# Banded masks added by identity matmuls in a windowed-attention block, with three loads and steps moved

## The reference

```python
rel = kj - BLOCK - qi                                             # key pos - query pos
valid = (jnp.abs(rel) <= WINDOW)[None] & (kpos >= 0) & (kpos < L)
s_loc = jnp.where(valid[None, :, None, None], s_loc, NEG_INF)
logits = jnp.concatenate([sink_l, s_ctx, s_loc], axis=-1)
probs = jax.nn.softmax(logits, axis=-1).astype(v.dtype)
```

## Time and profile before

| | |
|---|---|
| median of 3 runs | 1018.33 us (1017.56 to 1018.68) |
| profiled execution | 1016.99 us; span of its slowest core 1015.4 us |
| spans of the 8 cores | 1011.6 to 1015.4 us |
| PE busy | 900.5 us, 89% of the span |
| DVE, ACT, POOL busy | 487.6, 297.3, 247.4 us (48%, 29%, 24%) |
| chain that ended last | PE 77%, DVE 5%, DMA 5%, issue 5%, ACT 3%, POOL 2% |
| largest lines of that chain | L1051 29%, L916 16%, L1186 14%, L947 5%, DMA of `wu` 5% |

### The profile page before, as it was taken

How to read it: one execution, slowest core, us unless ns; L and a number is a source line. 1 busy time by engine, 2 the same in 40 slices (tenths; PEclk the granted TensorE clock), 3 DMA queues, 4 the chain that set the end, 5 groups by cost and what they waited for, 6 DMA issues and landing times.

```text
span 1015.4 us, 15294 instructions; the slowest of 8 cores (1011.6 to 1015.4 us)
## 1 busy us (share of the span) xinstructions
PE 900.5 (89%) x5291; PEld 439.2 (43%) x5369; DVE 487.6 (48%) x946; ACT 297.3 (29%) x408; POOL 247.4 (24%) x282
## 2 busy tenths in 40 slices
PE   1537897878779999999998999999999999999993
PEld 0314454444444444444444444444444444444443
DVE  2135565467772255556666522122121123777775
ACT  2214545567772223343333321111111111000000
POOL 6021342263741235545544204000000000000000
PEclk9988999988799999999999999999999999999997
DMA  8998285069302012212931309982222003332331
GB/s 172 188 223 199 84 166 115 2 110 181 106 23 104 1 42 85 70 55 84 184 118 53 83 1 137 168 128 45 42 42 41 1 1 104 125 125 93 115 104 43
DMA packets 41068, 95.48 MB, mean 94 GB/s; under 512 B 4000, under 2 KB 4512, under 8 KB 40992
## 3 DMA queue, kind: packets, MB, share of 16 engines
q0 software_dynamic: 21136, 40.44, 25.5%
q1 hardware_dynamic: 19856, 54.06, 16.2%
HBM read 118.14 MB, written 16.78 MB: 133 GB/s over the span
## 4 chain that ended last, share of the span: by engine, by line
PE 77%; DVE 5%; DMA 5%; issue 5%; ACT 3%; POOL 2%; another core or an unknown queue 1%; DVEq 0%; ACTq 0%; POOLq 0%
PE bank L1051 29%; PE bank L916 16%; PE bank L1186 14%; PE bank L947 5%; DMA arena<-wu 5%; PE bank L544 2%; PE bank L477 2%; POOL arena L243 2%; PE bank L763 2%; PE bank L517 1%; ACT arena L766 1%; PE bank L786 1%; DVE arena L732 1%; PE bank L528 1%
## 5 line engine op out<-in xcount | busy, mean ns | idle before, releaser
L1051 PE MATMUL bank<-arena 128*128 128x512 bf16 x1378 | 303.5, 379 | 1.6
L1051 PEld LDWEIGHTS bank<-arena 128*128 128x128 bf16 x1408 | 137.7, 98 | 165.4
L1062 DVE TENSOR_TENSOR arena<-bank,arena 128x512 bf16<-128x512 f32 x88 | 60.9, 692 | 224.2 <-PE bank L1051 217.2
L916 PE MATMUL bank<-arena 128*128 128x512 bf16 x751 | 166.7, 379 | 0.9
L1186 PE MATMUL bank<-arena 128*128 128x512 bf16 (+1 forms) x735 | 151.5, 366 | 0.7
L1060 ACT ACTIVATE arena<-bank 128x512 f32<-128x512 f32 x88 | 52.4, 595 | 224.9 <-PE bank L1051 224.9
L916 PEld LDWEIGHTS bank<-arena 128*128 128x128 bf16 x768 | 75.0, 98 | 89.9
L1186 PEld LDWEIGHTS bank<-arena 128*128 128x128 bf16 x748 | 73.2, 98 | 79.1
L932 DVE TENSOR_TENSOR arena<-bank,arena 128x512 f32<-128x512 f32 x64 | 44.3, 692 | 94.3 <-PE bank L916 94.3
L766 ACT ACTIVATE arena<-bank 128x1024 bf16<-128x1024 f32 x80 | 77.3, 1030 | 21.5 <-PE bank L763 21.1
L925 ACT ACTIVATE arena<-bank 128x512 f32<-128x512 f32 x64 | 37.0, 591 | 118.9 <-PE bank L916 118.9
(11 more groups left out here) (108 smaller groups left out, 893.8 us busy)
## 6 DMA issues: line engine op xcount, KB each, us to landing
arena<-xh SPq DMA_DIRECT2D x34, 512.0 KB, 6.6
arena<-wada POOLq DMA_DIRECT2D x12, 1024.0 KB, 26.0
arena<-wff POOLq DMA_DIRECT2D x11, 1024.0 KB, 11.2
xmid_d<-arena SPq DMA_DIRECT2D x16, 512.0 KB, 2.9
arena<-xmid_d SPq DMA_DIRECT2D x16, 512.0 KB, 3.7
out<-arena SPq DMA_DIRECT2D x32, 256.0 KB, 2.0
arena<-wff POOLq DMA_DIRECT2D x11, 512.0 KB, 21.5
arena<-wout SPq DMA_DIRECT2D x16, 256.0 KB, 2.8
```

What stands on the lines that cost most here:

```text
L916: t_mm = S.op('pe', lambda e, k=k, n=n, p=bk(bank), lhs=w[:, lo + k, :], rhs=src[:, k, tok]: e.matmul(p, lhsT=lhs, rhs=rhs, start=(k == 0) ...
L1051: rhs=h2T[:, k, tok]: e.matmul(p, lhsT=lhs, rhs=rhs, start=(k == 0), stop=(k == 7)),
L1062: fb_free[b0 + 1] = sg_free[s_] = t_act[(f, tg)] = S.op('dve', lambda e, f=f, p=bk(b0 + 1), sg=sgb[s_]: e.tensor_tensor(out=act[f][:, tok] ...
```

## The change

Four things change, all before line 916.

1. The masks become numbers to add, 0 where a key is kept and -2^20 where it is not. `att_mask` is gone. For s = 0 and 2 `att_scores` first issues two matmuls of the identity with the mask (repeated over the four heads of a group) into the two banks, and the score matmuls accumulate onto them.
2. `att_turn(j)` takes bank 6 + j % 2, so that the transposes of tile j - 1 go to the bank that `gmlp_tile(j)` does not use.
3. `rope_load(1)` waits for `wvvb`.
4. The last two `p0_compute` move from tiles 1 and 3 of the loop to the 6th and 7th side step of the last projections, and each tile of the loop has one `wout_step`, from tile 0 to 15.

```diff
-    rope_load(1)
+    rope_load(1, t_wvvb)
...
-          3: [(ln_out, 4, LO, TB, t_mod)], 4: [(ln_turn, 4, HI, TB)], 5: [(ln_out, 4, HI, TB, t_mod)]}
+          3: [(ln_out, 4, LO, TB, t_mod)], 4: [(ln_turn, 4, HI, TB)], 5: [(ln_out, 4, HI, TB, t_mod)], 6: [(p0_compute,)], 7: [(p0_compute,)]}
...
+        masked = s in (0, 2)
+        if masked:
+            mi = (0 if j == 0 else 1) if s == 0 else (3 if j == NT - 1 else 2)
+            for kv in range(2):
+                S.op('pe', lambda e, psb=bk(2 * i2 + kv), mi=mi: e.matmul(
+                    psb, lhsT=ident, rhs=masks[:, mi:mi + 1, :].to_broadcast([128, 4, 128]), start=True, stop=False),
+                    deps=[s_free[i2], T_CONST] if kv == 0 else (), sig=False)
...
-            t_mm = S.op('pe', lambda e, psb=bk(2 * i2 + kv), ksrc=ksrc, kv=kv, j=j: e.matmul(
+            t_mm = S.op('pe', lambda e, psb=bk(2 * i2 + kv), ksrc=ksrc, kv=kv, j=j, first=not masked: e.matmul(
...
-                start=True, stop=True), deps=[s_free[i2], t_k, t_qg[j // 4]] if kv == 0 else (), sig=(kv == 1))
+                start=first, stop=True), deps=[s_free[i2], t_k, t_qg[j // 4]] if kv == 0 else (), sig=(kv == 1))
...
-    def att_mask(j, s):
-        slot = (j % 2) * 5 + s
-        mi = (0 if j == 0 else 1) if s == 0 else (3 if j == NT - 1 else 2)
-        att[j]['p'][s] = S.op('dve', lambda e, pt=PT[slot], mi=mi: e.tensor_tensor(
-            out=pt, in0=pt, in1=masks[:, mi:mi + 1, :].to_broadcast([128, 8, 128]), op=ALU.mult),
-            deps=[att[j]['p'][s], T_CONST])
...
-        b0 = 6 + (j + 1) % 2
+        b0 = 6 + j % 2
...
-            if j in (1, 3):
-                p0_compute()
-            if 4 <= j < 12:
-                wout_step(2 * (j - 4))
-                wout_step(2 * (j - 4) + 1)
+            wout_step(j)
...
+    off = np.float32(-2.0 ** 20)
+    full = np.full((128, 128), off, np.float32)
+    maskP, maskN = (1.0 - maskP) * off, (1.0 - maskN) * off
```

More of the change, by code:

```diff
@@ L827, in build_nc @@
         att_scores(0, m)
-        if m in (0, 2):
-            att_mask(0, m)
         qk_mm(m, 3, (4, 6))
@@ L848, in build_nc @@
         if nxt:
-            att_mask(j + 1, 0)
             att_scores(j + 1, 1)
@@ L857, in build_nc @@
             att_pv(j, 0, (2, 3))
-        if nxt:
-            att_mask(j + 1, 2)
         if cur:
@@ L1344, in prep_inputs @@
     maskN = (ki <= qi).astype(np.float32)
-    zero = np.zeros((128, 128), np.float32)
+    off = np.float32(-2.0 ** 20)
+    full = np.full((128, 128), off, np.float32)
+    maskP, maskN = (1.0 - maskP) * off, (1.0 - maskN) * off
     bc = lambda v: np.ascontiguousarray(np.broadcast_to(v[None, :], (128, v.shape[0])))
@@ L1362, in prep_inputs @@
         rc, rs = _rope_tables(start)
-        mk = np.stack([zero if seg == 0 else maskP, maskP, maskN, zero if seg == 3 else maskN], 1).reshape(128, 512)
+        mk = np.stack([full if seg == 0 else maskP, maskP, maskN, full if seg == 3 else maskN], 1).reshape(128, 512)
         m = dict(shared)
```

## The result

The changed kernel takes **1010.82 us** (median of 4 runs, 1009.0 to 1012.09) against 1018.5 for the kernel before (1017.56 to 1018.99): ratio 0.9924 with an interval of 0.9907 to 0.9942, so 5.9 to 9.5 us faster. The forecast was 1007.0.

A forecast was written before the change was run, and what follows sets the result against it. It took transfers to bound the start, TensorE the projections, and a chain of scores, exponential, mask, gMLP read and transposes the loop. Terms -3.5 + 3.4 - 10.7 - 0.5 = -11.3 gave a median of 1007.0 us, range 999.5 to 1015.

The forecast's parts named there:

- part 1: Start of the kernel: the second rope pair waits for wvvb, which then lands earlier; -3.5 us (bounds 0 and -6.3).
- part 2: End of the projections: two p0_compute moved there cost matmuls and a wait for bank 7; +3.4 us.
- small edits: Scores before the loop gain from masks leaving VectorE, weight-scaling steps count as nothing; -0.5 us (-2 to +0.9).
- Part 3: Attention loop: masks as identity matmuls, transposes in the other bank; 82 us against 92.7, so -10.7 us.
- The two additions to it: Attention loop, on top of 78 us: 2.9 us for lower clock, 1 us for a wait behind POOL's wc1 loads.
- x tile 0 comes at about 86 + 5 = 91: Group 2's first x tile, queued behind the put-off 1.8 MB, lands near 91 us, the fourth near 100.
- I keep 3.5 of the 6 us: Of 6.0 us gained where wvvb lands, 3.5 remain after VectorE's stop for group 2's x tiles.
- (c): Rival at the start: the rope wait gives nothing, all is paid back at the x tiles; +3.5, 1010.5 us; chance 0.09.
- (a): Rival in the loop: the clock stays as before, 24 us at the lower level; loop -5, 1012.7 us; chance 0.18.
- (d): Rival in the loop: TensorE still waits for VectorE, now at gMLP; 6 us a tile, 1015 us; chance 0.06.
- (e): Rival in the loop: slower, 64 more matmuls make TensorE the bound at 1.2 GHz; 1039 us; chance 0.07.
- (b): Rival in the loop: weight-scaling steps hold POOL, 5.65 us a tile for eight tiles; +3.6, 1010.6 us; chance 0.10.

The follow-up runs named there:

- the second measurement: The unmodified changed kernel once more, against the kernel before on a second chip: 1009.86 us, ratio 0.9897.
- 1: The changed kernel without the second rope pair's wait for wvvb: 1009.88 us, ratio 0.9904.
- 2: The changed kernel with both moved p0_compute back in tiles 1 and 3 and the old weight-scaling schedule: 1008.98 us, ratio 0.9893.
- 3: The kernel before with only the masks as identity matmuls and the transposes in the other bank: 1008.88 us, ratio 0.9887.
- experiment 8: The changed kernel, gate rows and constants requested behind group 2's x tiles, moved p0_compute in banks 1 and 3, no rope wait: 1012.41 us, ratio 0.9899.
- 5: The kernel before with only the transposes in the other bank, masks still on VectorE: 1012.3 us, ratio 0.9915.
- 7 (again): The changed kernel, gate rows and constants behind group 2's x tiles, moved p0_compute in banks 1 and 3, on another chip: 1011.17 us, ratio 0.9883.
- 10: The changed kernel with only the two moved p0_compute in banks 1 and 3 instead of 6 and 7: 1014.33 us, ratio 0.9944.
- kernel 7: The changed kernel, gate rows and constants behind group 2's x tiles, moved p0_compute in banks 1 and 3; first measured at 1001.26 us, ratio 0.9813.

## Why the prediction was right, and where it was not

The sign, the main cause and the range were right; the size was 3.6 us too large (-11.3 forecast, -7.7 measured; -10.3 by the second measurement). That it came so near is in part luck: the loop gave 2.6 us more than forecast (-13.3 by the means), while the projections (part 1 and part 2, -0.1 forecast, +3.6 measured) and the small edits (1.7) gave 5.4 less. Line 916's matmuls begin 8.5 us earlier by the means, not 11.

- **Part 3, -10.7 forecast, -13.7 measured on core 2** (-12.7 by the means). The tile is 5.32 us in the steady part (5.2 forecast), bound by ScalarE and the hand-overs at the two bank pairs. The two additions to it did not come: no time at the lower clock (2.9 forecast) and no wait behind POOL's `wc1` requests (1; the gMLP matmuls waited 0.3). The 8 us at the lower clock were a choice between two ends, and the end with none was right. The rule quoted there (the Trainium skill, TensorE: Matmul & The Clock Gate, Part 1: activity releases the throttle) gave 13.7, and the trace agrees with it on the core that the forecast was made for, 92.7 to 79.0 us.
- **Part 1, -3.5 forecast, nothing measurable.** The step that failed is "x tile 0 comes at about 86 + 5 = 91". `wvvb` came at 69 to 72 as said, but the first x tile on the eight cores only at 93.3 to 97.6 and the fourth within 4 to 5 us of it, near 100 as forecast. I had counted 16 us for the put-off 1.8 MB and 5 for the tile alone; on core 7 the 1.8 MB took 24 (requested from 71.1 on, the last landed at 95.0) and the first tile came 2.6 behind them, as POOL's weights came beside them (by the DMA view 75% of the engines' time from 68 to 90 us, SP's requests 30%). "It stops some 3 us" became 8.43 us on VectorE, TensorE's 1.83 us of waiting for the copy behind it became 6.16, and its clock fell. "I keep 3.5 of the 6 us" became 2.4 of 5.2 by the means just behind that wait, and the lower clock took most of the rest. That is the step of rival (c); that its 1010.5 is so close to 1010.82 is chance, as other terms were off too. The rule quoted there (the Trainium skill, DMA: Bandwidth & Descriptors, "Issuing engines are not separate DMA queues") gave 0 for part 1; experiments 1 to 3 agree with it for this change, while experiment 8 shows 2.0 to 2.5 us for the wait where the put-off bytes delay nothing that is needed soon.
- **Part 2, +3.4 forecast, about +4.4 at the place** (1 against 3), and 1.5 to 1.7 more on the five cores where the clock fell behind it. The two matmul groups and the wait for the second one's additions came as worked out (1.68 against 1.4). Left out was the first step's bank: bank 6 waits 1.05 us for `ln_out`. The removal from the loop gives back 2.0 us (1 against 3, the schedule of the weight scaling included), so the move loses about 2 us; the ratios of 1 and 3 (0.9904 and 0.9887) say the same, though their intervals overlap.
- **Small edits, -0.5 forecast, +1.2 measured** between L658 and the loop. Where the clock stays up behind L658 it is 23.4 on core 2 (184.5 to 207.9) against 23.2, so no gain at the first scores; the rest is the clock behind the wait at L658, on core 7 (1.51 and 1.92 above) and not on core 2, where the same wait of 1.68 was followed by 1.05 and 1.04 at a granted clock of 1.00. The weight-scaling steps cost nothing that shows: the loop is 83.2 us with one in every tile. No experiment moved them alone.
- **The slowest core, not in the sum at all, +1.5 between the two profiles.** The time is that of the core on which the stops and the clock fall worst. This varies from execution to execution more than between the kernels (3.6 us above the mean before, 4.1 and 3.2 in the changed kernel, on average), so it is no effect of the change that the runs show; what sets it stays open.

Of the rivals, (a), (d) and (e) were wrong for this change; (d)'s wait is real where the bank is changed without the masks (5). (b) did not show: the loops of the changed kernel took 83.2 to 84.7 us on every core.

## What to carry to other kernels

When requests are held back to free the DMA engines for an urgent load, look at what stands behind them in the same in-order queue: hold back only what nobody needs soon, and let the next urgent tiles pass first. A step moved to a busy engine's chain costs its own time plus the wait for its buffer, so read who last touched that buffer at the new place. Where two edits work on the same chain, test each alone: here either gave most of the loop's gain, and only with one of them did TensorE's clock stay up.

## What the hardware showed that was not expected

A third level of the granted clock. In experiments 7 (again), 8 and 10, on one chip, two neighbouring cores were held for 150 us; kernel 7 on core 6 and then on core 5 of one execution:

```profile
core 6: us, PE busy (x) PEld busy (x) DVE busy (x) ACT busy (x) POOL busy (x), PEclk, DMA share, GB/s
88.00:238.00 150.00, 140.31 (x1019) 69.93 (x1029) 75.02 (x179) 77.58 (x106) 53.86 (x73) 0.81 0.51 105
238.00:289.00 51.00, 47.99 (x636) 24.90 (x637) 28.33 (x106) 46.33 (x49) 26.17 (x22) 1.00 0.66 129
```

```profile
88.00:238.00 150.00, 135.05 (x1185) 71.39 (x1183) 80.30 (x202) 87.86 (x118) 59.45 (x77) 0.98 0.58 120
238.00:289.00 51.00, 46.12 (x614) 24.58 (x611) 28.40 (x105) 41.43 (x43) 25.19 (x22) 1.00 0.47 96
```

Core 6 was granted 0.81, neither of the two levels, and afterwards 1.00 at a TensorE that is as busy; its span is 1009.6 us against 993.9. The compared executions of the kernel before on that chip (1016.67 to 1023.61 us) have no such pair of cores, and no other profile has such a stretch; that of the changed kernel shows 0.82 and 0.81 for 6 to 15 us near 550 us, on all eight cores. The Trainium skill (TensorE: Matmul & The Clock Gate, Part 1) tells of a current limiter that takes a whole die to 13/16 of the clock and holds it while the load lasts. The level agrees (13/16 is 0.8125), and near 550 us so do the whole dies (cores 0 to 3 and 4 to 7); from 88 to 238 us two cores of a die were held and not four, and they were let go while the load lasted. What sets it off stays open, and whether the changed kernel itself meets it on that chip was not tried. So version 7 beats both kernels on the chip of 5 to 7 by more than the intervals, and on the chip of 8 to 10 the kernel before (0.9883, 0.9835 to 0.9932).
